# A hybrid decoder layer on one core: last stage with a place for each chunk, first tiles by halves, routing turned from the plain sum

## The reference

```python
    h = rms_norm(x, norm1_w)
    x = x + hybrid_mixer(h, w_in, ...)
    h = rms_norm(x, norm2_w)
    g_prob = softmax(tokens @ rg_w + rg_b)          # top 1 of 4 groups
    e_p, e_local = top_k(softmax(e_logits), 2)      # top 2 of the group's 8 experts
    hid = silu(xblk @ w_gate[e]) * (xblk @ w_up[e]) # 32 experts, 1024 -> 512 -> 1024
    x = x + sum of the two weighted expert outputs
    return rms_norm(x, final_norm_w)
```

## Time and profile before

| | us |
|---|---|
| median of 3 runs (2199.6 to 2202.0) | 2200.93 |
| the profiled execution | 2209.94 |
| its span | 2208.2 |
| TensorE busy | 1995.4 (90%) |
| VectorE busy | 1327.4 (60%) |
| ScalarE busy | 929.1 (42%) |
| GpSimd busy | 360.3 (16%) |

### The profile page before, as it was taken

One profiled execution on the slowest core, in us unless ns is written; L12 is line 12 of the kernel. 1 busy time (PEld: TensorE's weight loads), 2 busy tenths in 40 slices (PEclk: granted clock), 3 DMA queues, 4 the chain that ended last, 5 costly groups with the idle time before them and its releaser, 6 DMA issues. The chain is left out here.

```text
span 2208.2 us, 25315 instructions
## 1 busy us (share of the span) xinstructions
PE 1995.4 (90%) x10102; PEld 1661.2 (75%) x10103; DVE 1327.4 (60%) x1429; ACT 929.1 (42%) x1004; POOL 360.3 (16%) x199
## 2 busy tenths in 40 slices
PE   4999999999989999999897899985699999999970
PEld 3778888888978777877776688774588888888850
DVE  4640000566215777868774565555699999899945
ACT  5120101111113444444443234231678888787742
POOL 3213323233310000000000000011122222222210
PEclk9999999999999999999998999997799999999995
DMA  5133222133226556656554764451899999999947
GB/s 155 60 135 114 96 95 84 50 114 118 92 87 155 145 134 131 156 147 146 130 134 150 265 213 176 167 200 48 301 367 385 388 386 382 391 389 384 390 170 266
DMA packets 220173, 435.86 MB, mean 197 GB/s; under 512 B 30802, under 2 KB 153698, under 8 KB 192546
## 3 DMA queue, kind: packets, MB, share of 16 engines
q1 hardware_dynamic: 186946, 356.72, 48.1%
q10 hardware_dynamic: 22240, 56.63, 7.0%
q0 software_dynamic: 10880, 21.03, 2.5%
HBM read 369.67 MB, written 81.43 MB: 204 GB/s over the span
## 5 line engine op out<-in xcount | busy, mean ns | idle before, releaser
L583 DVE TENSOR_SCALAR tap<-u,taps 128x1024 f32<-128x1024 f32 x16 | 20.1, 1298 | 294.2 <-ACT u L541 294.2
L613 PE MATMUL ps<-h_hi,w_hi 128*128 128x512 f32 x576 | 178.4, 391 | 4.8 <-PEq L58 4.8
L613 PE MATMUL ps<-h_lo,w_hi 128*128 128x512 f32 x576 | 178.3, 391 | 0.0
L613 PE MATMUL ps<-h_hi,w_lo 128*128 128x512 f32 x576 | 178.2, 391 | 0.0
L2336 DVE TENSOR_TENSOR gu_lo<-gate_raw,gu_hi 128x2048 fp32r<-128x2048 f32 x64 | 146.7, 2293 | 32.3 <-ACT gu_hi L2280 32.3
L1249 PE MATMUL psum<-h_hi,l_hi 128*128 128x512 f32 x384 | 159.0, 414 | 7.3 <-PEq L58 7.3
L1249 PE MATMUL psum<-h_lo,l_hi 128*128 128x512 f32 x384 | 160.6, 418 | 0.0
L1249 PE MATMUL psum<-h_hi,l_lo 128*128 128x512 f32 x384 | 158.4, 413 | 0.0
L2336 DVE TENSOR_TENSOR gu_lo<-up_raw,gu_hi 128x2048 fp32r<-128x2048 f32 x64 | 146.5, 2288 | 16.7 <-ACT gu_hi L2280 16.7
L2341 DVE TENSOR_TENSOR dn_lo<-dn_raw,dn_hi 128x2048 fp32r<-128x2048 f32 x62 | 142.0, 2292 | 16.0 <-ACT dn_hi L2290 13.0
L551 ACT ACTIVATE out<-ps 128x2048 f32<-128x2048 f32 x14 | 26.4, 1883 | 271.3 <-PE ps L613 202.3
(11 more groups left out here) (356 smaller groups left out, 4912.1 us busy)
## 6 DMA issues: line engine op xcount, KB each, us to landing
gate_raw<-moe SPq DMA_DIRECT2D x66, 1024.0 KB, 8.7
up_raw<-moe SPq DMA_DIRECT2D x64, 1024.0 KB, 8.2
dn_raw<-moe SPq DMA_DIRECT2D x62, 1024.0 KB, 7.8
w_raw<-w_in SPq DMA_DIRECT2D x26, 1024.0 KB, 6.7
dn_raw<-w_br SPq DMA_DIRECT2D x15, 1024.0 KB, 7.5
l_raw<-w_gates ACTq DMA_DIRECT2D x24, 512.0 KB, 5.2
s_gates<-l_out ACTq DMA_DIRECT2D x48, 256.0 KB, 3.8
gate<-s_gates SPq DMA_DIRECT2D x16, 768.0 KB, 5.5
```

What stands on the lines that cost most here:

```text
L613: ins = nc.tensor.matmul(ps[b][:, a * T + half * 512:a * T + half * 512 + 512], w[:, k, a * P:(a + 1) * P], h[:, k, half * 512:half * 512 ...
```

## The change

- **Start.** `x_in` has four buffers (two are the later `keys`), loaded from SP and ScalarE. The casts of h move from ScalarE to GpSimd; the rests of `va` and of the first two weight pairs move from GpSimd to VectorE. The first three tiles are made by halves: chunks 0 to 3 of all three, with the transposes of chunks 5 to 7 between their matmuls, then chunks 4 to 7.
- **Borders.** The last stores of the first stage and of projection are waited for in the next stage. The mixers' two small loads come first in SP's queue.
- **Merging.** SP issues all first pieces of y in their order.
- **Routing.** Rows are transposed from the sum x2; the norm's weight is multiplied into the router's matrix, and VectorE multiplies the logits with the row's inverse root. For chunks 0 to 3 h2 gets a buffer of its own. Turns and logits of a chunk stand inside the next chunk's projection. Chunks 6 and 7 are picked one by one. The record's row is rank·32 + expert, and `recs` is one transfer.
- **Finish.** Each chunk has its own place: four in the experts' weight buffers and four new ones. Final weights and x2 of the last chunks are loaded into `dn_raw` during the last expert, the pairs of chunks 0 to 3 at its end, the rest in the stage of further slabs. For chunks 1, 3, 4 and 6 TensorE adds the two rows in PSUM with an identity, in full fp32. SP issues the stores.

The diff, cut to its core:

```diff
@@ norm1_and_decays
+        NX = 4
+        x_in = [sb(f"x_in{b}", [P, D]) for b in range(NX - 2)] + keys
...
+            for c in [c for c in range(NCH) if c >= NX or c % 2 == 0]:
+                if c >= NX:
+                    sp.wait_ge(xn_ready, c - NX + 1)
+                x_rows(sp, c)
...
+            def upper_part(c):
+                pool.wait_ge(hf_ready, c + 1)
+                nc.gpsimd.tensor_copy(h_hi[:, :, c * CH:(c + 1) * CH], h_f[c % 2][:]).then_inc(hi_ready, 1)
...
-            def upper_part(c):
-                act.wait_ge(hf_ready, c + 1)
-                nc.scalar.copy(h_hi[:, :, c * CH:(c + 1) * CH], h_f[c % 2][:]).then_inc(hi_ready, 1)
...
-            for b in range(2):
-                act.wait_ge(qk_stored[b], 16 * QK_T // 2)
...
+            FIRST = 3
+            TURNS = {(0, 4): NCH // 2 + 1, (1, 2): NCH // 2 + 2, (2, 0): NCH // 2 + 3}
...
+            for c in range(NCH // 2 + 1):
+                turn(c)
+            for half in range(2):
+                pe.wait_ge(h_ready, NCH // 2 * (half + 1))
+                for q in range(FIRST):
...
+                    half_tile(q, half, *((v_hi, v_lo) if q == 0 else (w_hi[0][:, :, ws], w_lo[0][:, :, ws])))
@@ mixers
+            project_stored(sp)
             load_v(0)
@@ merge_and_route
-    BATCHES = ((0, 4), (4, 2), (6, 2))
+    BATCHES = ((0, 4), (4, 2), (6, 1), (7, 1))
...
-            places = dr["table"].rearrange("(e s) w -> s e w", s=T)[0:SLAB]
-            sp.dma_start(recs[:, 0:2, :], places[:, 0:2, :]).then_inc(recs_first, 16)
-            sp.dma_start(recs[:, 2:N_EXPERTS, :], places[:, 2:N_EXPERTS, :]).then_inc(recs_in, 16)
+            sp.dma_start(recs[:], dr["table"].rearrange("(s e) w -> s e w", e=N_EXPERTS)[0:SLAB]).then_inc(recs_in, 16)
...
-                tt(lg[:, c, :], lg_ps, rb[:], ALU.add).then_inc(lg_in, 1)
+                stt(lg[:, c, :], lg_ps, stat[:, 1, c:c + 1], rb[:], ALU.mult, ALU.add).then_inc(lg_in, 1)
...
+            tt(rw[:], rw[:], n2_col[:].unsqueeze(2).to_broadcast([P, KT, NL]), ALU.mult).then_inc(rw_ready, 1)
...
-                    pe.wait_ge(h2_ready, i + 1)
-                    if i == 0:
-                        pe.wait_ge(x2_ready, 1)
+                    pe.wait_ge(x2_ready, i + 1)
...
+            for c in range(HC + 1, NCH):
+                out_chunk(c, 0, 2)
+                if c == NCH - 1:
+                    rank(1)
+                turn_both(c - 1)
+                out_chunk(c, 2, 5)
+                logits(c - 1)
+                out_chunk(c, 5, KT)
+            turn_both(NCH - 1)
+            rank(2)
+            logits(NCH - 1)
+            rank(3)
@@ experts_first_slabs, SP
+            for b in range(2):
+                sp.wait_ge(scattered[b], 16 * N_EXPERTS // 2)
+            sp.dma_start(todo[:], dr["work"].rearrange("(o n) w -> o (n w)", o=1)).then_inc(todo_in, 16)
+            for c in range(GU):
+                sp.dma_start(pairs[c], pair_rows(dr, c)).then_inc(pairs_in[c], 16)
@@ finish
+                        ins = nc.tensor.matmul(both[n][:, hs], ident[:], pairs[c][:, a, hs], start=a == 0, stop=a == 1)
...
+                nc.vector.tensor_tensor(x2[c], x2[c], two, ALU.add).then_inc(sum_ready, 1)
...
-                act.wait_ge(y_ready, c + 1)
-                act.dma_start(out[c * CH:(c + 1) * CH, :], rows[b][:, 2, :]).then_inc(stored[b], 16)
```

More of the change, by code:

```diff
@@ L92, in wait_past, with norm1_and_decays @@
         eng.wait_ge(sem, value)
-def norm1_and_decays(nc, io, dr, ident, h_hi, h_lo, w_raw, w_hi, w_lo):
+def norm1_and_decays(nc, io, dr, ident, h_hi, h_lo, w_raw, w_hi, w_lo, x_n, qk_stored):
     HF_T = WIDTHS["hf"] // P
@@ L400, in _, with half_tile @@
                 ins.then_inc(xT_ready, 1)
-            pe.wait_ge(h_ready, NCH)
+            FIRST = 3
+            TURNS = {(0, 4): NCH // 2 + 1, (1, 2): NCH // 2 + 2, (2, 0): NCH // 2 + 3}
+            def half_tile(q, half, hi, lo):
+                hs = slice(half * 512, half * 512 + 512)
+                for k in range(KT):
+                    if half == 0 and (q, k) in TURNS:
+                        turn(TURNS[q, k])
+                    for w, h in ((hi, h_hi), (hi, h_lo), (lo, h_hi)):
+                        ins = nc.tensor.matmul(acc[q][:, hs], w[:, k, :], h[:, k, hs], start=k == 0 and w is hi and h is h_hi,
+                                               stop=k == KT - 1 and w is lo, skip_group_check=True)
+                if half:
+                    ins.then_inc(mm_done, 1)
             def tile(q, hi, lo):
@@ L467, in project @@
         out_ready = sem("out_ready")
-        stored = [sem(f"stored{b}") for b in range(2)]
         pad_ready = sem("pad_ready")
@@ L2575, in finish @@
         y_ready = sem("y_ready")
-        stored = [sem(f"stored{b}") for b in range(NB)]
+        stored = sem("stored")
         dve_own = sem("dve_own")
```

366 lines of the change are left out of this document (208 added, 158 removed).

## The result

The changed kernel takes **2149.67 us** (median of 4 executions, 2147.8 to 2150.6), the kernel before beside it 2201.26 (2199.6 to 2202.0). The ratio is 0.976, interval 0.974 to 0.979: 51.6 us less, by the interval 47 to 58. The forecast was 2145 us, 56 less. The profiled execution of the changed kernel has a span of 2148.1 us, 60.1 less than the one of before. So the two traces differ by more than the medians do; where that comes from is the first question of the experiments.

What follows compares the result with a forecast made beforehand. TensorE is filled nearly everywhere, so only its idle or cold places can gain: 18 + 2.2 + 4 + 5 + 1 + 4.5 + 3 + 18.3 = 56 us off 2200.9 gives 2145 us; 8-in-10 range 2134 to 2163.

Steps and rivals of the forecast that it cites:

- The base of the sum: Whole kernel: profiled execution is 9 us above the median 2200.93, differences are waits and carry over, so 56 comes off 2200.9.
- "clock" term: Start of the mixers: TensorE's clock falls while it waits for small loads; 2 us of 3.4 taken back (0 to 3).
- Start: First stage (norm1_and_decays): half tiles begin at 24.3 us, third tile done at 63 against 81.2; gain 18 us (10 to 20).
- Borders: After first stage and after projection: stores' landing no longer waited for; gains 2.2 (1 to 3) and 4 us (2.5 to 4.5).
- The small loads and the clock: Start of the mixers: two small loads now first in the queue, gain 3 us, and less slow clock, gain 2.
- End of routing: Last chunks' choice to reading of the records: last sum some 4 us later, records read at about 1539; gain 4.5 us (1 to 7).
- Finish: Last stage: loads asked for earlier, four sums on TensorE, end at 2189.9 instead of 2208.2; gain 18.3 us (12 to 21).
- Rival (a): First stage and mixers: gains run into VectorE's decay chain or first chunk's loads; gain 40, 2161 us; chance 14%.
- Rival (b): Last stage: TensorE's sums run cold after over 15 us idle; gain 50, 2151 us; chance 9%.
- Rival (c): First stage: GpSimd's casts hold VectorE's rests, eight of 1.03 us, start gives 10; 2153 us; chance 6%.
- Rival (d): Borders: the barrier waits for another engine's work, so borders give nothing; 2151 us; chance 6%.
- rival (e): Expert loop: weight buffers at other addresses slow the transfers; at 12% longer experts the kernel takes 2214 us; chance 2%.

Runs made afterwards that it cites:

- the borders' run: Changed kernel with the last stores of the first stage and of projection waited for at the end of their own stage again; 2162.92 us, ratio 0.983.

## Why the prediction was right, and what was off

The direction, the size and the places were right: 51.6 us against 56, inside the range. Some of the closeness is luck: against the second trace of before, the start and its border gave 5.8 us less than forecast and routing 2.3 less, while the experts' start and the last stage gave 2.5 more. The sum against what the runs showed, step by step:

- **The base of the sum** was misread. The step was "these differences are waits and carry over": the profile's stretches were taken for those of a typical execution, though it stood 9 us above the median. It held falls of the clock in filled stages (at 105, 950 and 1075 us) that a second profile of the same kernel did not have. The terms were read from its idle times and not from its stretches, so only the "clock" term of 2 us rests on them; but a reader who checks the forecast against the two traces finds 60.1 us, 4 too many, for the same reason.
- **Start.** Forecast 18, at the third tile's eviction; measured there 14.0 (67.31 against 81.27), and 14.2 to 15.5 at the narrow matmuls. The mechanism (halves) is right: without them nothing is gained. Two terms were too small: the first chunk is turned 1.0 us later, at 8.69 instead of 7.67; and the rests beside GpSimd's casts, taken at 1.23 each, had 2.06, 1.77 and 2.88. First half-tile matmul 27.91 instead of 24.3. A fall of the clock behind the narrow matmuls, 3.2 us whole and 1.6 short, then takes part of it back in both traces of the changed kernel; the sum had no term for it.
- **Borders.** 2.2 and 4 forecast; idle time fell from 4.78 to 2.44 and from 7.30 to 3.45, TensorE restarts 1.34 and 1.51 us behind the last store's issue, as said. The small loads and the clock, 5: the mark 50 us into the mixers comes 5.0 sooner (4.2 and 5.8 in the two traces), the whole stage is 4.6 shorter against the second trace. The runs that undo one edit at a time cost 12.5 and 6.0 us, so each costs more than its own term when it alone is undone.
- **Merging.** 1 forecast, nothing seen; the stretch varies by 5 us between executions.
- **End of routing.** 4.5 forecast; 3.1 by the eight traces at 88.0, 2.3 by the mean of two. From the last sum to the records it takes 22.3 us, as worked out (30.8 before). The last sum itself comes 5.3 us later and not 4, for the reason named, the sixth chunk's choice; the run that moves the sum into the choice gets 2.1 back.
- **Start of the experts.** 3 forecast, 3.9 measured.
- **Finish.** 18.3 forecast, 20.1 measured. VectorE's first wait is 4.15 us (3.7 said), the first matrix sum 6.68 (6.8 said for a cold one), the next 3.60 (3.5). The stage begins 0.7 us later than before relative to the scatter, where 2 were taken for the eight issues.

Rival (a) did not come: VectorE's eviction at 67.31 waits for nothing, but TensorE has no idle time between 28 and 138 us. Rival (b) came in part (the first sum only). Rival (c) came with 2 to 3 of its 8 us; the forecast went by the one row that seemed to speak against it, and had read only half of that row's place. Rival (d) is refuted by the borders' run, rival (e) by the experts' stretch, which is within 3 us of before.

## What to carry to other kernels

Where a stage begins behind a chain over many chunks, give the matrix engine the first half of several tiles as soon as half the chunks are there: it was worth 14 to 15.5 us here where it acts, 12 at the end of the stage and 9.6 in the median. A wait at a border can cost more than its length, since the next stage's transfers and evictions shift against each other: 12.5 us for 6.2 us of idle time here. When a row is taken as evidence that one engine does not hold another, look at both engines' timelines at that place. Profile a kernel twice before taking the length of a filled stretch from one trace, compare the profiled execution's time and granted clock with those of the timed ones, and read terms from idle times.

## What the runs showed of the hardware

- The clock of TensorE falls to half in some executions and not in others, at the same place of the same program. Behind the four 16-partition fp32 matmuls of the first stage, seven of fourteen traces have a fall that costs 3.2 us, three a shorter one of 1.6, four have none. Beyond its first 60 us the mixers' stage has none to two.
- Over 48 executions of the kernel before, time and mean granted clock go together: 2206.9 to 2209.8 us at 0.958, 2195.6 to 2200.3 at 0.962 and 0.963.
- Contention of VectorE and GpSimd goes both ways: a cast of 128×1024 took 1.04 us alone and 1.97 beside a subtraction, a subtraction 1.22 alone and up to 2.88 beside casts, a two-input operation of the convolution 1.28 alone and 2.92 beside a cast.
- With one transfer of 4096 pieces of 16 bytes ahead of it the first expert's matmul came 6.7 us later, counted from that transfer, than with 128 runs of 512 bytes (22.8 against 16.2 us, one trace).
